# The first mixer's attention steps taken two at a time, with two heads side by side on TensorE's array

## What is computed

```python
h = rmsnorm(x, g_mix[l])
proj = h @ w_in[l]
q_d, k_d, v_d, q_s, k_s, v_s, gate_d, gate_s = split_cols(proj, IN_WIDTHS)
y_dil = dilated_attention(...)     # 24 heads of 64: 3 dilation groups of 8 heads, merged by their lse
y_swa = swa_sink_attention(...)    # 16 query heads, 2 key heads, window 128, with sinks
mixed = (jax.nn.sigmoid(gate_d) * (y_dil @ w_br_dil[l])
         + jax.nn.sigmoid(gate_s) * (y_swa @ w_br_swa[l]))
x = x + mixed @ w_out[l]
```

## Time and profile before

| | us |
|---|---|
| median of 3 runs | 1798.34 (1798.18 to 1803.49) |
| the profiled execution | 1793.65 |
| its span, first to last instruction | 1791.8 |
| TensorE busy in it | 1686.8 (94%) |
| VectorE, ScalarE busy | 1288.9 (72%), 1026.5 (57%) |
| the stage of the 32 steps, about | 152 to 285 |

### The profile page before, as it was taken

One profiled execution on the slowest core, in us unless ns is written; L12 is line 12 of the kernel. 1 busy time (PEld: TensorE's weight loads), 2 busy tenths in 40 slices (PEclk: granted clock), 3 DMA queues, 4 the chain that ended last, 5 costly groups with the idle time before them and its releaser, 6 DMA issues.

```text
span 1791.8 us, 29597 instructions
## 1 busy us (share of the span) xinstructions
PE 1686.8 (94%) x11478; PEld 1499.8 (84%) x11478; DVE 1288.9 (72%) x1439; ACT 1026.5 (57%) x1127; POOL 63.9 (4%) x56
## 2 busy tenths in 40 slices
PE   8999989889999999999989879899999999799998
PEld 7998878878877666677758769799998999799997
DVE  6545688675589999999987867575555888575554
ACT  4333465454678999999977354354334484343432
POOL 0000000000000000000006400000000020000000
PEclk9999999989999999999999989999999999999999
DMA  9562114065799999999996424246554555255540
GB/s 324 186 188 72 48 60 157 8 269 201 246 369 418 418 419 419 420 420 419 420 397 228 144 95 142 78 158 208 177 180 133 169 192 189 71 166 187 187 140 24
DMA packets 194960, 391.74 MB, mean 219 GB/s; under 512 B 6960, under 2 KB 152112, under 8 KB 178480
## 3 DMA queue, kind: packets, MB, share of 16 engines
q1 hardware_dynamic: 193200, 383.89, 59.1%
q0 software_dynamic: 1664, 6.52, 1.0%
HBM read 379.77 MB, written 10.62 MB: 218 GB/s over the span
## 4 chain that ended last, share of the span: by engine, by line
PE 61%; DMA 15%; DVE 14%; issue 6%; ACT 3%; DVEq 0%; SPq 0%; POOL 0%; ACTq 0%; POOLq 0%
DMA raw<-w_e_up_dram 13%; PE ps L664 10%; PE ps L665 10%; PE ps L669 10%; DVE wlo L1901 6%; PE ps L1000 3%; PE ps L821 3%; PE ps L892 2%; PE ps L890 2%; PE ps L898 2%; PE ps L959 2%; PE ps L953 2%; PE ps L845 2%; PE ps L955 2%; ACT whi L1328 2%
## 5 line engine op out<-in xcount | busy, mean ns | idle before, releaser
L1901 DVE TENSOR_TENSOR wlo<-raw,whi 128x2048 fp32r<-128x2048 f32 (+3 forms) x358 | 813.7, 2282 | 226.0 <-ACT whi L1328 219.6
L1328 ACT ACTIVATE whi<-raw 128x2048 fp32r<-128x2048 f32 (+3 forms) x358 | 675.5, 1891 | 340.9 <-PE ps L669 196.5
L664 PE MATMUL ps<-xh,whi 128*128 128x256 f32 x800 | 200.8, 291 | 11.9 <-DVE xl L1914 10.8
L665 PE MATMUL ps<-xl,whi 128*128 128x256 f32 x800 | 198.0, 287 | 0.0
L664 PE MATMUL ps<-xb_h,whi 128*128 128x256 f32 x768 | 186.9, 284 | 5.2 <-DVE arena L1983 5.2
L665 PE MATMUL ps<-xb_l,whi 128*128 128x256 f32 x768 | 186.4, 284 | 0.0
L664 PEld LDWEIGHTS ps<-xh,whi 128*128 128x128 f32 x800 | 156.2, 195 | 13.9 <-issue 11.6
L953 PE MATMUL ps<-whi,xh 128*128 128x512 f32 x528 | 160.7, 397 | 0.0
L665 PEld LDWEIGHTS ps<-xl,whi 128*128 128x128 f32 x800 | 156.5, 196 | 0.2
L664 PEld LDWEIGHTS ps<-xb_h,whi 128*128 128x128 f32 x768 | 147.4, 192 | 5.6 <-DVE arena L1983 5.6
L959 PE MATMUL ps<-wlo,xh 128*128 128x512 f32 x528 | 143.8, 397 | 6.6 <-DVE wlo L1901 5.2
(11 more groups left out here) (429 smaller groups left out, 2883.7 us busy)
## 6 DMA issues: line engine op xcount, KB each, us to landing
raw<-w_e_gate_dram SPq DMA_DIRECT2D x64, 1024.0 KB, 10.7
raw<-w_e_up_dram SPq DMA_DIRECT2D x64, 1024.0 KB, 10.7
raw<-w_e_down_dram SPq DMA_DIRECT2D x64, 1024.0 KB, 10.7
raw<-ffn_w_gate_up_dram SPq DMA_DIRECT2D x44, 1024.0 KB, 5.1
raw<-w_in_dram SPq DMA_DIRECT2D x30, 1024.0 KB, 5.8
raw<-ffn_w_down_dram SPq DMA_DIRECT2D x22, 1024.0 KB, 4.9
raw<-xa_w_kv_dram SPq DMA_DIRECT2D x16, 1024.0 KB, 5.6
raw<-xa_w_q_dram SPq DMA_DIRECT2D x8, 1024.0 KB, 5.3
```

What stands on the lines that cost most here:

```text
L664: nc.tensor.matmul(o[b], wh, h, start=b == 0 and a == 0, stop=False, skip_group_check=True)
L665: nc.tensor.matmul(o[b], wh, l, start=False, stop=False, skip_group_check=True)
L1328: nc.scalar.activation(whi[u % HL][:, 0:n], raw[u % RAW][:, 0:n], ACT.Copy).then_inc(hi_ready, 1)
L1901: v.tensor_tensor(wlo[u % HL][:, 0:n], raw[u % RAW][:, 0:n], whi[u % HL][:, 0:n].bitcast(F32), ALU.subtract).then_inc(lo_ready, 1)
```

## The change

The order of the dilated steps becomes: pair of heads, half of the queries, head; so two steps that follow one another are two heads with the same queries, one on either half of the partitions. Window steps keep their order. Every engine gets an `attend_two` that takes the steps in pairs.

- TensorE: scores of the next pair (`score_two`, heads in turn), then for both steps of the pair the transposes and a quarter of a gate unit (`fourth_unit`: 12 matmuls), then the mix of both (`mix_two`, halves in turn, always into bank 4). A pair's scores over 256 keys lie in banks 0, 5 and 1, and the last of them waits for the first (`third_scored`), since both write bank 1.
- ScalarE: copies of both steps, exponentials of both steps of the next pair, then `between` of both.
- VectorE: probabilities of both, output of the pair before, bias and maximum of both steps of the next pair, then `between` of both.
- ScalarE takes a gate unit out, and makes the next high half, at step 4k+3 in place of 4k+2. VectorE's low half stays at 4k+3.

```diff
         def score_bank(step, g):
-            at = g * T if len(step["scores"]) == 3 else g * 512
-            return ps[:, at // 512, at % 512:at % 512 + step["nk"]]
+            if step["kind"] == "dil":
+                bank, at = 5 * step["head"], g * T
+                if step["nk"] == P:
+                    bank, at = step["head"], g * P
+                elif g == 2:
+                    bank, at = 1, step["head"] * T
+            else:
+                bank, at = g, step["qt"] * T if step["kind"] == "swa" else 0
+            return ps[:, bank, at:at + step["nk"]]
...
-                for hh in range(DIL_HEADS):
-                    lo = HD * (hh % 2)
-                    for qt in range(2):
+                for pair, qt, head in product(range(DIL_HEADS // 2), range(2), range(2)):
+                        hh, lo = 2 * pair + head, HD * head
...
+            def fourth_unit(u, part):
+                _, kc, n = units[u]
+                if part == 0:
+                    st["bank"] = lin_bank()
+                    weights_in(u)
+                b, ks = part // 2, range(part % 2 * kc // 2, (part % 2 + 1) * kc // 2)
...
+            def score_two(p):
+                two = steps_a[2 * p:2 * p + 2]
+                if p >= 1:
+                    pe.wait_ge(att_biased, 2 * p)
+                if two[0]["kind"] == "dil":
+                    turns = ((0, 2), (1, 0), (0, 0), (1, 1), (0, 1), (1, 2))
+                else:
+                    turns = ((0, 0), (0, 1), (1, 0), (1, 1))
+                shared = two[0]["kind"] == "dil" and two[0]["nk"] > P
+                for n, (a, g) in enumerate(turns):
+                    q, k = two[a]["scores"][g][0]
+                    if n == 5 and shared:
+                        pe.wait_ge(third_scored, st["third"])
+                    mm = nc.tensor.matmul(score_bank(two[a], g), q, k, start=True, stop=True)
+                    if n == 0 and shared:
+                        st["third"] += 1
+                        mm.then_inc(third_scored, 1)
+                mm.then_inc(att_scored, 2)
+
+            def mix_two(p, PT):
+                two = steps_a[2 * p:2 * p + 2]
+                pe.wait_ge(att_pt, 2 * p + 2)
+                if st["y"] >= 1:
+                    pe.wait_ge(att_out, st["y"])
+                if two[0]["kind"] == "dil":
+                    groups = [[(0, 0), (1, 0)]]
+                else:
+                    groups = [[(0, 0), (0, 1)], [(1, 0), (1, 1)]]
+                for group in groups:
+                    n = len(two[group[0][0]]["pv"][0][2])
+                    for a in range(n):
+                        for b, i in group:
+                            lo, _, pv = two[b]["pv"][i]
+                            v, g, kt = pv[a]
+                            at, per = two[b]["qt"] * P, two[b]["nk"] // P
+                            mm = nc.tensor.matmul(ps[lo:lo + HD, 4, at:at + P], v, PT[b][:, g * per + kt, :],
+                                                  start=a == 0, stop=a == n - 1)
+                mm.then_inc(att_mixed, 2)
+                if two[1]["last"]:
+                    st["y"] += 1
+
+            def attend_two(PT, between):        # TensorE
+                n = len(steps_a) // 2
+                score_two(0)
+                for p in range(n):
+                    if p + 1 < n:
+                        score_two(p + 1)
+                    for a in (2 * p, 2 * p + 1):
+                        turn(a, steps_a[a])
+                        between(a)
+                    mix_two(p, PT)
...
             def gates_between(a):
-                if a % 2 == 0:
-                    feature_unit(u_in[23 + a // 4], half=a % 4 // 2)
+                fourth_unit(u_in[23 + a // 4], a % 4)
...
+            def attend_two(PT, between):        # ScalarE
+                n = len(steps_a)
+                exps(0, steps_a[0])
+                exps(1, steps_a[1])
+                for s in range(0, n, 2):
+                    copy_turned(s, steps_a[s], PT)
+                    copy_turned(s + 1, steps_a[s + 1], PT)
+                    if s + 2 < n:
+                        exps(s + 2, steps_a[s + 2])
+                        exps(s + 3, steps_a[s + 3])
+                    between(s)
+                    between(s + 1)
...
-                if a % 4 == 2:
+                if a % 4 == 3:
                     u = u_in[23 + k]
                     ahead(u)
                     evac(u, st["lin"], sg[:, 2 * k:2 * k + 2, :])
...
+            def attend_two(y_of, between):      # VectorE
...
+                bias_max(0, steps_a[0])
+                bias_max(1, steps_a[1])
+                for s in range(0, n, 2):
+                    probs(s, steps_a[s])
+                    probs(s + 1, steps_a[s + 1])
+                    if s:
+                        out(s - 1)
+                    if s + 2 < n:
+                        bias_max(s + 2, steps_a[s + 2])
+                        bias_max(s + 3, steps_a[s + 3])
+                    between(s)
+                    between(s + 1)
+                out(n - 1)
```

More of the change, by code:

```diff
@@ L14 @@
 from contextlib import ExitStack
+from itertools import product
 import numpy as np
@@ L415, in attention @@
                         steps.append(dict(nk=nk, qt=qt, scores=sc, bias=bi, merged=True, sink=None, scale=0.125,
-                                          pv=[(lo, 0, pv)], last=hh % 2 == 1 and qt == 1,
+                                          kind=kind, head=head, pv=[(lo, 0, pv)], last=hh % 2 == 1 and qt == 1,
                                           y=[qd[:, hh // 2, :]]))
@@ L432, in attention @@
                         steps.append(dict(nk=nk, qt=qt, scores=sc, bias=bi, merged=False, sink=2 * c, scale=0.125,
-                                          pv=pv, last=qt == 1, y=[qs[:, c, :]]))
+                                          kind=kind, pv=pv, last=qt == 1, y=[qs[:, c, :]]))
             elif kind == "mla":
@@ L443, in attention @@
                         steps.append(dict(nk=nk, qt=qt, scores=sc, bias="causal", merged=False, sink=None,
-                                          scale=float(QK) ** -0.5, pv=pv, last=qt == 1, y=[my[:, c, :]]))
+                                          kind=kind, scale=float(QK) ** -0.5, pv=pv, last=qt == 1, y=[my[:, c, :]]))
             else:
@@ L451, in attention @@
                         steps.append(dict(nk=T, qt=qt, scores=sc, bias=None, merged=False, sink=None,
-                                          scale=float(XA_HD) ** -0.5, pv=pv, last=qt == 1, by_key=l == 0,
+                                          kind=kind, scale=float(XA_HD) ** -0.5, pv=pv, last=qt == 1, by_key=l == 0,
                                           y=[xq[:, 2 * h, :], xq[:, 2 * h + 1, :]]))
@@ L643, in _ @@
         def _(pe):
-            st = dict(lin=0, sq=0, step=0, xl=0, y=0, fresh=False)
+            st = dict(lin=0, sq=0, step=0, xl=0, y=0, fresh=False, third=0)
             def high_in(u, i=None, step=6):
@@ L717, in feature_unit @@
                 if half == 1:
+                    mm.then_inc(unit_used, 1)
+            def fourth_unit(u, part):
[4 more added lines that the diff above has]
+                b, ks = part // 2, range(part % 2 * kc // 2, (part % 2 + 1) * kc // 2)
+                wh, wl = wview(whi, u, kc, n), wview(wlo, u, kc, n)
+                mm = triple(st["bank"][:, b, :], [(wh[:, k, b * P:b * P + P], wl[:, k, b * P:b * P + P], xh[:, k, :],
+                                                   xl[:, k, :]) for k in ks],
+                            first=part % 2 == 0, last=part % 2 == 1)
+                if part == 3:
                     mm.then_inc(unit_used, 1)
@@ L867, in gated @@
+            def attend_two(PT, between):
[8 more added lines that the diff above has]
+                    mix_two(p, PT)
+                st["step"] += len(steps_a)
             def gated(p0, n, trio):
@@ L1456, in attend @@
                 st["step"] += len(steps)
+            def attend_two(PT, between):
[10 more added lines that the diff above has]
+                    between(s + 1)
+                st["step"] += n
             def experts(p0):
@@ L1678, in gates_out @@
                     st["lin"] += 1
-            attend(steps_a, PT_first, gates_out)
+            attend_two(PT_first, gates_out)
             split_highs(qs, u_in[-1] + 1)
@@ L2127, in attend, with out @@
                 st["step"] += len(steps)
+            def attend_two(y_of, between):
+                n = len(steps_a)
+                def out(s):
+                    if steps_a[s]["last"]:
+                        dve.wait_ge(att_mixed, s + 1)
+                        v.tensor_copy(y_of(st["y"], 1)[:, 0, :], ps[:, 4, 0:T]).then_inc(att_out, 1)
+                        st["y"] += 1
+                bias_max(0, steps_a[0])
[11 more added lines that the diff above has]
+                out(n - 1)
+                dve.wait_ge(att_out, st["y"])
+                st["step"] += n
             def experts(p0):
```

5 lines of the change are left out of this document (3 added, 2 removed).

## The result

| | before | after |
|---|---|---|
| median of 5 runs, us | 1798.34 (1795.95 to 1803.49) | 1813.06 (1810.88 to 1815.74) |
| span of the profiled execution | 1791.8 | 1811.2 |
| first dilated transposes, us from the start | 162.1 | 157.64 |
| first transposes of the last two steps | 279.6 | 286.2 |
| last output copy of the stage ends | 284.90 | 293.63 |

The ratio is 1.0079 [1.0065, 1.0093], so the changed kernel is slower by more than 0.3%. The forecast was 1807 with a range from 1794 to 1819.

A forecast was written before the change was run, and what follows sets the result against it. TensorE was taken to bound the dilated steps, the loop over VectorE and ScalarE the window steps. 1793.65 + 3.8 (waits) + 5 (clock) = 1802.5 us, 1807 on the median's scale; range 1794 to 1819.

The forecast's parts named there:

- The step that decides: Low half of the gate weights: VectorE's subtraction waits for ScalarE's conversion, seven waits over 3 us each, 3.3 in dilated pairs.
- TensorE's part: Dilated steps: a pair's scores and mix cost what one head's did; four steps about 13.7 us in place of 17.91.
- Window pairs: Seven window pairs: 5.9 without subtraction, 10.8 or 8.9 with one or the dilated split, 57.1 us in all.
- The tail: Last pair: VectorE waits for the conversion ahead of the last output copy, which ends 7.7 us later, at 288.7.
- The sum of the stage: Whole attention stage: 3.8 us longer from the waits, plus 5 us from the clock.
- The clock: TensorE at half clock behind new idle gaps: 1.5 us for each of three, 0.5 for two of about 3 us; 5 us.
- the rival of more half-clock stretches: Half clock also behind dilated gaps of 2.3 us, or twice as long each: 1816 us; chance 0.12.
- The waits are there, the clock stays: Rival: the stage's waits add 3.8 us and TensorE's clock does not fall: 1802 us, no change; chance 0.22.
- No wait at the subtraction: Rival: ScalarE converts while VectorE is still at its biases; some 19 us less, 1779; chance 0.16.
- Heads that don't overlap: Rival, dilated pairs: the array's halves don't run side by side in the new order; 9 us more, 1816; chance 0.07.
- My rule that a shift of the stage's end passes one to one: After the attention stage: everything hangs on it, so a shift of its end moves the whole time by as much.

The follow-up runs named there:

- early conversion: Changed kernel with ScalarE making the next high half between its two copies of a pair, ahead of the exponentials; 1775.2 us, again 1777.14.
- the gaps filled: Changed kernel with filler matmuls on TensorE, results unused, in the seven idle gaps behind the subtraction; 1802.15 us, ratio 1.0012.

## Why the prediction was right

**The step that decides** held. Seven waits of 2.48 to 4.90 us stand where I put them (I had said over 3 each; the short one is at the unit of half the size), and the one of the last pair, 3.02, too. In the dilated steps they are 3.7 to 3.9 against my 3.3. The early conversion removes them and the loss with them. A dilated pair with the subtraction takes 9.83 (forecast 10.1); the two pairs together 16.6 to 16.7 (16.1 before the clock; 15.8 with the gaps filled). The second pair's transposes start at 163.96 (164.0).

**TensorE's part** held, a little too cautious. Two sides in turn do cost what one did: 24 mix instructions take 1.53 us, 12 one-sided ones took 1.52. With no waits two dilated pairs take 12.7 us where I had 13.7, of which the even pair is 5.35 for 5.9. By the Trainium skill, TensorEngine Tiling (Array Packing), "PSUM Bottleneck", packing leaves the emptying of PSUM as it was, which may become the bound. In the dilated stretch of the early kernel TensorE is still the bound, with 16.99 of 17.00 us busy against VectorE's 15.30, so the margin is small.

**Window pairs.** Forecast 57.1 us for the seven; with the gaps filled they took 57.0, so close because single ones were off both ways: up to 1.1 more with a subtraction (11.27, 11.92 and 9.34 for 10.8, 10.8 and 8.9) and up to 0.8 less without. The 11.92 began in the half-clock stretch that was left. In the changed kernel itself they took 61.0, with the clock's part in it. The tail was 7.4 for 7.7. TensorE's gaps ahead of window pairs were 4.61, 5.59 and 5.30 us for my 4.3 to 4.9.

**The sum of the stage.** Forecast: 3.8 for the waits and 5 for the clock, 8.8. Measured: 8.7, as 1.8 and 6.9. Both terms are off by 2 us, and the errors cancel: that the sum is right to 0.1 us is luck.

**The clock.** The direction was right, the place only half. I gave the long gaps ahead of window pairs 1.5 us each and the dilated gaps of 2.3 nothing. The three dilated gaps of 2.49 us (the first ends at 173.79, the next at 190.34) were followed by 3.4 us at 1.2 GHz as well, and behind two of the long gaps it was 6.8 us and not 3.4 (from 241.8 and from 262.2). That was the rival of more half-clock stretches, and it came out in part: 6.9 us and not its 9.5. By the Trainium skill, TensorE: Matmul & The Clock Gate, "Why this matters for your kernels", idle gaps between bursts bring the array back to the half clock, where the page speaks of gaps longer than these dilated ones. Behind the gaps of 4.61, 5.59 and 5.30 us the trace agrees, with 0.50 granted; behind the shorter ones it shows 0.50 as well, and there the measurement decides. With filled gaps the clock stays at 1.00 through the dilated steps. It is not a fixed price: in the second profile of the changed kernel the stretch from 163 to 181 us ran at full clock, gap and all, and a gap of 2.97 us left it alone in the earlier trace rows.

**The rivals.** "The waits are there, the clock stays" is what the filled gaps imitate, and it gave 1802.15 where I had worked out 1802. Part of that is luck too: the stage is 1.8 us longer and not 3.8, and the kernel before took 1800.54 beside that run. "No wait at the subtraction" did not happen by itself; made on purpose it gave 1775.2, where the rival's sum said 1779. Heads that don't overlap did not occur; given by head they overlap in part and cost 7.5 us.

**What is left.** 1813 is 6 above 1807; the second measurement of the changed kernel, 1810.59, is 4 above. In the profiled executions some 3 of it lie between the stage's end and the experts' first gather. Windows of that part, first after, then before:

```profile
293.63:378.37 84.74, 71.09 (x531) 68.55 (x529) 58.77 (x111) 38.63 (x53) 0.57 (x1) 0.88 0.25 81
```

```profile
284.90:366.71 81.81, 68.79 (x546) 66.60 (x544) 58.75 (x111) 38.52 (x53) 1.01 (x2) 0.95 0.27 85
```

The second profiles repeat it (84.79 and 81.84). It is the same work at a lower clock (0.88 against 0.95). My rule that a shift of the stage's end passes one to one left this out. It isn't that a later end makes this part longer: the early kernel has 81.82 in one profile and 83.25 in the other, and the kernel with the dilated split a pair later, whose stage ends first of all (259.7), has 84.52. Why the clock falls more often there in some executions stays open. The other 3 us are within the 9 by which the rest differs from one execution to the next.

## What to carry to other kernels

When steps are merged, look at the in-order engines for work that stood between two steps and now stands behind both: a request for which a second engine waits belongs ahead of the work that this same engine has just released. Here one call moved ahead of the exponentials turned 0.8% slower into 1.4% faster than before. The order of pieces on TensorE is only worth what it covers: gates in four parts cost 14 us with steps one by one, and with steps in pairs it was the halves that cost 12 to 14.

## What the runs showed of the hardware

- Two one-sided runs of twelve, given one after the other on different halves of the array, took 2.45 us; given in turn 1.53; one alone 1.52.
- In one execution three gaps of 2.49 us in TensorE's work each had 3.4 us at 1.2 GHz behind them; in another of the same kernel the first of the three left the clock alone.
- Ten matmul instructions on constants in each dilated gap (2.4 us) kept the clock at 2.4 GHz in the dilated steps. With nine matmuls (eighteen instructions) in each window gap behind a subtraction too, the kernel was 8 to 11 us faster, with the waits all in place.
